# Seven row tiles of a projection phase finished inside the attention that follows

## The reference, cut to what matters

```python
q, k, v, xq = split_cols(h @ w_in, [nh * DIL_HEAD_DIM] * 3 + [D_XA])      # nh = 12 heads of 128
q = apply_rope(rms_norm(hs(q), q_norm), cos, sin)
k = apply_rope(rms_norm(hs(k), k_norm), cos, sin)
for g, (window, dilation) in enumerate(DIL_GROUPS):                       # (128,1), (512,4), (2048,16)
    o, lse = dilated_window_attention(q[g], k[g], v[g], window, dilation)
o = softmax-weighted sum of the three groups
xa = memory_cross_attention(xq, mem_n, xa_w_kv[i], xa_q_norm[i], xa_k_norm[i])   # 4 heads of 64, 256 keys
x = x + concatenate([o, xa]) @ w_out
```

## Time and profile before

| | |
|---|---|
| median of 3 runs | 2404.55 us (2403.34 to 2406.7) |
| the profiled execution | 2405.09 us, its span 2403.3 us |
| PE, DVE, ACT, POOL busy | 2338.1 us (97%), 1888.7 us (79%), 1105.6 us (46%), 221.4 us (9%) |
| seven-block phase, last product | ends at 1514.9 us of the span |
| the first attention on PE | 1527.92 to 1594.02 us |

### The profile page before, as it was taken

The page is one execution under the profiler, slowest core; times in us unless marked ns, Lnnn a source line. Parts: engine busy times, 40 slices in busy tenths (PEclk is TensorE's granted clock), DMA queues, the critical chain, the costliest instruction groups (busy, mean ns, idle before and its releaser), DMA issues. The chain is left out here.

```text
span 2403.3 us, 33350 instructions
## 1 busy us (share of the span) xinstructions
PE 2338.1 (97%) x11988; PEld 2030.3 (84%) x11988; DVE 1888.7 (79%) x2917; ACT 1105.6 (46%) x2217; POOL 221.4 (9%) x252
## 2 busy tenths in 40 slices
PE   8999999999999999999999999798999999999998
PEld 7998877888888888778999999787888888888877
DVE  4422574479999999997998888766779999998996
ACT  6433553344444443446455555665344444444443
POOL 1010012000000002202111111303000000000000
PEclk9999999999999999999999999899999999999999
DMA  4230122222222238963433333745622222227863
GB/s 156 88 98 18 43 86 62 88 72 88 79 79 79 91 112 298 316 199 110 132 113 110 115 106 110 241 139 155 202 82 79 82 94 79 88 79 277 291 184 127
DMA packets 253660, 303.42 MB, mean 126 GB/s; under 512 B 49544, under 2 KB 192888, under 8 KB 253496
## 3 DMA queue, kind: packets, MB, share of 16 engines
q1 hardware_dynamic: 249336, 301.27, 38.2%
q10 hardware_dynamic: 4160, 0.02, 0.1%
HBM read 230.13 MB, written 71.11 MB: 125 GB/s over the span
## 5 line engine op out<-in xcount | busy, mean ns | idle before, releaser
L52 PE MATMUL psum<-f_T_lo 128*128 128x512 f32 x616 | 242.1, 393 | 3.5 <-DVE f_T_lo L698 3.0
L53 PE MATMUL psum<-f_T_lo 128*128 128x512 f32 x616 | 239.9, 389 | 0.0
L54 PE MATMUL psum<-f_T_lo 128*128 128x512 f32 x616 | 239.8, 389 | 0.0
L52 PEld LDWEIGHTS psum<-f_T_lo 128*128 128x128 f32 x616 | 115.6, 188 | 34.5 <-DVE f_T_lo L698 10.8
L52 PE MATMUL psum<-hT_hi,f_up_hi 128*128 128x512 f32 x352 | 137.3, 390 | 0.4 <-DVE f_up_lo L637 0.4
L54 PE MATMUL psum<-hT_hi,f_up_lo 128*128 128x512 f32 x352 | 137.0, 389 | 0.0
L53 PE MATMUL psum<-hT_lo,f_up_hi 128*128 128x512 f32 x352 | 137.0, 389 | 0.0
L54 PEld LDWEIGHTS psum<-f_T_lo 128*128 128x128 f32 x616 | 115.6, 188 | 24.2
L53 PEld LDWEIGHTS psum<-f_T_lo 128*128 128x128 f32 x616 | 115.7, 188 | 23.2
L52 PE MATMUL psum<-p_operand,T_hi 128*128 128x384 f32 x384 | 129.2, 337 | 3.2 <-DVE p_operand L2196 2.5
L54 PE MATMUL psum<-p_operand,token_sums_lo 128*128 128x384 f32 x384 | 128.8, 336 | 0.0
(11 more groups left out here) (501 smaller groups left out, 6674.5 us busy)
## 6 DMA issues: line engine op xcount, KB each, us to landing
raw<-in_ffn_w_up_dram SPq DMA_DIRECT2D x88, 512.0 KB, 4.7
activations<-f_act SPq DMA_DIRECT2D x44, 512.0 KB, 2.6
f_up_pieces<-activations SPq DMA_DIRECT2D x30, 512.0 KB, 5.0
rows_w<-in_b_w_in_dram SPq DMA_DIRECT2D x24, 512.0 KB, 3.8
f_up_pieces<-in_ffn_w_down_dram SPq DMA_DIRECT2D x22, 512.0 KB, 4.8
rows_h<-group_rows SPq DMA_DIRECT2D x14, 768.0 KB, 5.7
group_rows<-raw SPq DMA_DIRECT2D x55, 192.0 KB, 1.8
x_between<-XY SPq DMA_DIRECT2D x16, 512.0 KB, 5.0
```

The costliest lines, as they stand in the source:

```text
L52: nc.tensor.matmul(out, lhs_hi, rhs_hi, start=start, stop=False)
L53: nc.tensor.matmul(out, lhs_hi, rhs_lo, start=False, stop=False)
L54: return nc.tensor.matmul(out, lhs_lo, rhs_hi, start=False, stop=stop)
```

## The change

Tiles 9 to 15 of the last chunk are no longer rotated, scaled and stored in the phase. They stay in their ring slots (tiles 9 to 11 already squared, with their root taken), and the class `LeftOver` treats them inside the first attention: DVE rotates left-over tile n after its other work of step 3n + 2 (steps 2, 5, ... 20), ACT squares the four unsquared ones in steps 3, 5, 7, 9 and scales tile n in step 3n + 4 (4, 7, ... 22), POOL takes two roots behind `CrossNorm`, and SP stores tile n after output tile 2n + 1, and the last three at the end. The k tables are loaded again for them (`left.load`, 2 x 512 KB) into two token tiles of `XY`, behind the stores of tiles 4 and 5. The wait for all stores moves from the opening of the attention to its end. `slots`, `operand0` and `rows_g` get their place in SBUF outside of the phase.

```diff
-LAST_ROTATED_IN = {3: (0, 1), 4: (2, 3), 5: (4, 5), 6: (6, 7, 8, 9, 10, 11), 7: (12, 13, 14, 15)}
+LAST_SQUARED_IN = {2: (0, 1, 2, 3), 5: (4, 5, 6, 7), 6: (8, 9, 10, 11)}
+LAST_ROTATED_IN = {3: (0, 1), 4: (2, 3), 5: (4, 5), 6: (6, 7, 8)}
-LAST_SCALED_IN = {4: (0, 1), 5: (2, 3), 6: (4, 5), 7: (9, 10, 11), 8: (12, 13, 14, 15)}
+LAST_SCALED_IN = {4: (0, 1), 5: (2, 3), 6: (4, 5)}
+LEFT_OVER = (9, 10, 11, 12, 13, 14, 15)
...
                 if m == LASTM - 1:
+                    sp.wait_ge(p_done, product(CH - 1, W22))
+                    left.load(sp)
                     for q in SCALED_LATE:
                         store(CH - 1, q)
                 if m == LASTM:
-                    sp.wait_ge(p_done, product(CH - 1, W22))
...
+class LeftOver:
+    FIRST_SQUARE = 3
...
+    def act(self, act, i):
+        n = (i - 3) // 2 + self.FIRST_SQUARE
+        if i % 2 and self.FIRST_SQUARE <= n < len(LEFT_OVER):
...
+                ins = self.nc.scalar.activation(self.squares_room[:, cols], self.slot(n)[:, cols], ACT.Square, accum_out=self.sums[:, s, 2 * j + h:2 * j + h + 1])
+        n = (i - 4) // 3
+        if i % 3 == 1 and 0 <= n < len(LEFT_OVER):
+            act.wait_ge(self.roped, n + 1)
+            if n >= self.FIRST_SQUARE:
+                act.wait_ge(self.rooted, s + 1)
...
+                ins = self.nc.scalar.activation(self.slot(n)[:, cols], self.slot(n)[:, cols], ACT.Copy, scale=self.rstd[:, s, 2 * j + h:2 * j + h + 1])
+    def dve(self, dve, i):
+        n = (i - 2) // 3
+        if i % 3 != 2 or not 0 <= n < len(LEFT_OVER):
+            return
+        if n == 0:
+            dve.wait_ge(self.loaded, 32)
...
+        for two in range(2):
+            ins = self.nc.vector.tensor_tensor(y[:, :, two, :], x[:, :, 1 - two, :], s[:, 1 - two, :].unsqueeze(1).broadcast_to([P, 2, P // 2]), ALU.mult)
...
+        self.nc.vector.tensor_tensor(heads, heads, self.cos[:, tile].unsqueeze(1).broadcast_to([P, 2, P]), ALU.mult).then_inc(self.turned, 1)
+        dve.wait_ge(self.turned, n + 1)
+        self.nc.vector.tensor_tensor(rows, rows, self.cross(n), ALU.add).then_inc(self.roped, 1)
...
                 if tiles.cross and i == CrossNorm.AT:
                     tiles.cross[2].dve(dve)
+                if left:
+                    left.dve(dve, i)
...
                 tiles.act_next(act, i)
+                if left:
+                    left.act(act, i)
...
                 tiles.cross[2].pool(pool)
+                left.pool(pool)
```

More of the change, by code:

```diff
@@ L1869, in rows_phase @@
                squares_room, small,
-               first_rows, rows_loaded, xq_load, ident, qT, kT):
+               first_rows, rows_loaded, xq_load, ident, qT, kT, first_operand, slot_room, left):
     DH = DC // 2
@@ L1970, in squared_in @@
         def squared_in(m):
-            return due(SQUARED_IN, SQUARED_IN, m)
+            return due(SQUARED_IN, LAST_SQUARED_IN, m)
         def rotated_in(m):
@@ L2312, in _ @@
             for c in range(CH):
-                for quads in ROOTS:
+                for quads in ROOTS if c + 1 < CH else ROOTS[:5]:
                     n, width = root_number(c, quads[0]), 2 * len(quads)
@@ L2489, in dve_next, with attention_phase @@
             self.dve_keys(dve, self.job(i)[0])
-def attention_phase(nc, ph, psum, ident, units, stage, turns_of, row_loads, loads=(), ahead=None, room=(), merge=None):
+def attention_phase(nc, ph, psum, ident, units, stage, turns_of, row_loads, loads=(), ahead=None, room=(), merge=None, left=None, left_store=None):
     U = len(units)
@@ L2690, in _ @@
                 row_loads(sp, t)
+                if left:
+                    for n in range(t // 2, (t + 1) // 2):
+                        left_store(sp, n)
                 if merge and t == 1:
@@ L2699, in _ @@
                 stage.store_sums(sp)
+            if left:
+                for n in range(TT // 2, len(LEFT_OVER)):
+                    left_store(sp, n)
         if ahead is not None:
@@ L4064, in build @@
             rooms = [rows_w[:, i, :].rearrange("p (d n) -> p d n", d=DC // 2) for i in range(4)]
+            with ExitStack() as same_place:
+                raw = sb("first_operand_sum", [P, 2, DC // 2, BLOCK], F32, same_place)
+            with ExitStack() as same_place:
+                x = sb("first_operand", [P, 2, DC // 2, BLOCK], F32R, same_place)
+            first_operand = x[:, 0, :, :], x[:, 1, :, :], raw[:, 1, :, :]
+            rows_g = sb("rows_g", [P, 2, 4 * BLOCK], F32, rows_ctx)
+            slot_room = sb("row_slots", [P, 3, BLOCK], F32, rows_ctx)
+            left = LeftOver(nc, c, raws, slot_room, small_room, squares_room, neg_half, XY[:, TT - 2, :], XY[:, TT - 1, :], tables_d[1])
             rows_phase(nc, "p1", psum, neg_half, hT_hi, hT_lo, h_room, T_hi, sum_lo, sum_room, rooms, raws, begun, w, order, tables_d, rows_d, xq_d, row_stored, squares_room, small_room, lambda t: row_load(0, t), rows_loaded[0],
-                       load_xq, ident, qT, kT)
-            rows_g = sb("rows_g", [P, 2, 4 * BLOCK], F32, rows_ctx)
+                       load_xq, ident, qT, kT, first_operand, slot_room, left)
             stage = Stage(nc, c1, order, outs_d, sums_d)
@@ L4072, in load_rows, with wait_rows, left_store @@
                 sp.dma_start(out, src).then_inc(rows_loaded[n % 2][t], 16)
+            def wait_rows(sp, groups):
+                for s in range(RING):
+                    sp.wait_ge(row_stored[s], 16 * len(range(s, TT + 16 * 2 * groups, RING)))
+            def left_store(sp, n):
+                left.store(sp, n, rows_d[len(order) - 1], row_stored)
+                if n == len(LEFT_OVER) - 1:
+                    wait_rows(sp, len(order))
             def loads_during(n):
@@ L4077, in first @@
                     if t < 0:
-                        for s in range(RING):
-                            sp.wait_ge(row_stored[s], 16 * len(range(s, TT + 16 * 2 * len(order), RING)))
+                        wait_rows(sp, 2)
                     else:
@@ L4117, in turns_of @@
                                      0 if n else TURNED_EARLY, qT, kT, cross)
-                    attention_phase(nc, f"da{n}", psum, ident, units, stage, turns_of, loads_during(n), loads, ahead, room, merge)
+                    attention_phase(nc, f"da{n}", psum, ident, units, stage, turns_of, loads_during(n), loads, ahead, room, merge,
+                                    left if n == 0 else None, left_store)
         up_ctx = ctx.enter_context(ExitStack())
```

59 lines of the change are left out of this document (56 added, 3 removed).

## The result

The changed kernel takes 2412.51 us (median of 7 runs, 2411.22 to 2414.71) against 2404.55 us (7 runs, 2403.34 to 2406.7): 8.0 us more. The ratio is 1.0032, with a 95% interval of 1.0021 to 1.0044. The profiled execution took 2411.91 us, with a span of 2410.1 us against 2403.3.

A forecast was written before the change was run, and what follows sets the result against it. PE, busy 97% of the span, was taken as the bound, so only its waits count. Nine added costs, 11.35 us, less 3.95 gained gave +7.4 on 2404.55: 2412.0 us, range 2404.0 to 2417.5.

The forecast's parts named there:

- the faster case: Rival: `cross_rows` land before 1525, POOL blocks nothing and rotations mostly fit into waits; 2398.5 us, chance 0.09.
- Items 1 to 5: Steps 2 to 5, in order: rotation 1.3, POOL block 2.3, ACT's square 0.35, rotation in key loop 1.3, POOL block 3.05 us.
- Items 1 and 2: Step 2: first rotation stands between sum and mask, 1.3 us; it also waits for POOL's product with the gain, 2.3 us.
- Item 5: Step 5: the second rotation falls inside POOL's second product and waits 3.05 us.
- Item 6: Steps 7 to 9: step 7's square and scaling, 1.2 us, exceed ACT's 0.85 us idle; 0.35 us, step 8's rotation nothing more.
- Items 7 to 9: Rotations: step 11, a key step, 1.3 us; step 14, 1.0 us; steps 17 and 20, 0.4 us at the most.
- item 9: Steps 17 and 20: the rotation's 0.6 us excess over DVE's 0.70 us idle spreads over the next step; 0.4 us at most.
- items 2, 5: Steps 2 and 5: rotations blocked by POOL's first and second products, 2.3 and 3.05 us.
- items 3, 6: ACT's added work: square ahead of an exponential in step 3, 0.35 us; square and scaling in step 7, 0.35 us.
- POOL does not hold up the rotations: Rival: rotations run beside POOL's two products, so both blocks fall away; 2406.6 us, chance 0.26.
- the power too: Rival: POOL's power of 32 columns also blocks the rotations, +5.45 us on the forecast; 2417.5 us, chance 0.09.
- The tables delay the transfer: Rival: the k table loads make `cross_rows` land 2.7 us later; 2414.7 us, chance 0.06.

The follow-up runs named there:

- late rotations: Changed kernel with the left-over rotations, squares and scalings moved to step 17 on, seven stores after the last output tile; 2402.55 us against 2405.69 for the kernel before.
- both repairs: Changed kernel with rotations, squares and scalings from step 17 on and `cross_rows` issued ahead of the `rows_x` loads; 2395.32 us against 2407.51 for the kernel before.
- the first experiment: Changed kernel with POOL's two products over the cross queries cut to 64 of 2048 columns; 2409.18 us against 2405.69 for the kernel before.

## Why the prediction was right, and where it was not

The forecast was 2412.0 and the measurement 2412.51; slower was the likeliest sign, and the two mechanisms, ACT's wait and the rotations behind POOL's products, are the ones that the runs show. That the number fits to 0.5 us is luck. From the landmark the gain ahead of the square was 1.5 us smaller than forecast and the cost behind it 1.0 larger, and a third attention shorter by 2.3, which nobody forecast, made up for both: +7.6 instead of +7.4.

**The start.** Predicted 8.6 us earlier, with `cross_rows` landing 3.95 us earlier, since it is issued so much earlier in SP's queue. From the landmark they were 8.14 and 2.41. In four of the six executions with the changed end of the phase SP issued the first load behind the store of tile 8 at 308.7 us, as worked out (1515.07 is 308.75), and the attention started at 312.4 to 312.6; in two, this one among them, both came 1 us later. So 1 us of the missing 1.5 lies within that scatter; 0.5 is the transfer, which took 12.3 us from issue to landing and not the 11.8 assumed. In absolute times the square at 1529.38 looks like a hit; 1.2 us of it is that the landmark stood earlier in this execution. ACT's wait grew to 7.31, not 5.3: in the profile's own times PE's first scores came 0.7 us sooner than the 1519.3 worked out, ACT was through with steps 0 and 1 in 3.5 us and not in 4.4, and the transfer came 0.4 later than 1529.0. That this wait is the next late thing was right; that moving the one load would nearly remove it was not seen. The prediction named the four `rows_x` loads ahead of it, but only to time the landing and as an argument against the faster case.

**Items 1 to 5, steps 2 to 5.** Counted from the end of ACT's square, the mask of step 6 came at 7.08 us before and 15.53 after: +8.45, where the items give 8.3. Items 1 and 2 hold: the first rotation ended 5.8 us after the square's end (6 predicted). Item 5 was 1.2 too large, with 1.88 us (2.36 - 0.48) instead of 3.05, because the copy ahead of it ended late, at 12.3 instead of 11.05. The likely reason is the cost taken at nothing, PE's lower clock: its work in steps 3 to 5 ran at 0.50, and what that cost was time that DVE would have been blocked in anyway. With `cross_rows` first, where PE was at 0.50 for a shorter time, the copy ended at 11.5 and item 5 measured 2.74.

**Item 6.** The key copy of step 11 stood at 17.04 before and 25.69 after, +8.65. The items up to 6 give 8.65.

**Items 7 to 9, and the clock.** The first maximum of a cross unit, 5 steps ahead of the one shown in the earlier trace rows, stood at 24.82 before (1559.74) and 35.65 after (1566.97): +10.83, where items 1 to 8 give 10.95. From there to the second attention the change added 1.5 us (36.66 - 35.14) and not the 0.4 of item 9. The second drop of the clock, at 1568 to 1571, falls there. The two experiments nearest to this kernel (POOL's products small, `cross_rows` first) had the same 1.61 us gap and no drop, and took 35.35 both. So item 9 measured 0.2, and the drop 1.3. The mis-sized term of the sum is thus the clock, bounded at 0 to 1 us and taken at nothing. No run switches the clock alone, so its share is read from the windows and from this comparison of profiles, and was not tested.

**The whole behind the square.** The stretches of the table take the 12.35 us apart:

| | us | from | forecast |
|---|---|---|---|
| rotations, their own time | 5.3 | POOL's products small, less no rotations | items 1, 4, 7, 8, 9: 5.3 |
| POOL's blocks | 4.1 | after, less POOL's products small, up to the first maximum | items 2, 5: 5.35 |
| ACT's squares and scalings | 1.1 | no rotations, less late rotations, up to the first maximum | items 3, 6: 0.7 |
| what the long wait leaves behind | 0.6 | late rotations, less both repairs, up to the first maximum | 0 |
| second drop of the clock | 1.3 | after, less POOL's products small, behind the first maximum | 0 |

The fourth row compares two kernels that differ by the order of the loads alone; behind the square the one with the long wait has PE at 0.50 for some 5 us and the other does not, so the lower clock is the likely cause. The rows form a chain of differences from the kernel after to the one before, and so add up to the whole; that each is worth the same in every kernel is an assumption.

**The third attention**, of which the prediction said that all that follows is shifted by the same. It gave back 2.3 us, and that hid the 2.5 (9.94 - 7.4) by which the second attention started later than forecast. Before, DVE's small merge products met POOL's splitting of `w_out`: 2.36 us beside POOL's 2.36, and just ahead of them 1.04 us for a maximum of 8 columns beside POOL's conversion of 1.04:

```profile
1652.63 1.04 DVE L3479 TENSOR_TENSOR merge_top<-merge_tops 128x8 f32<-128x8 f32 x1
```

```profile
1652.61 1.04 POOL L1168 CAST o_w_hi<-raw 128x1024 fp32r<-128x1024 f32 x1 [0.41 <-DMA raw<-in_b_w_out_dram]
```

After, POOL's operations stood elsewhere and the same maximum and the same three products took

```profile
1661.38 0.16 DVE L3583 TENSOR_TENSOR merge_top<-merge_tops 128x8 f32<-128x8 f32 x1
...
1661.77 0.32 DVE L3586 TENSOR_TENSOR merge_tops<-merge_tops,merge_top 128x8 f32<-128x8 f32 x3
```

between POOL's

```profile
1658.80 2.36 POOL L1170 TENSOR_TENSOR o_w_lo<-raw,o_w_hi 128x1024 fp32r<-128x1024 f32 x1
1662.50 1.04 POOL L1168 CAST o_w_hi<-raw 128x1024 fp32r<-128x1024 f32 x1 [1.34 <-DMA raw<-in_b_w_out_dram]
```

In the eight profiles the third attention lasts 48.4 to 48.9 us in the four where the three products took 2.36 or 2.37, and 46.5 to 46.7 in the four where they took 0.32. POOL's third piece waits for a load (0.3 to 0.5 us in the first four, 1.3 to 1.8 in the others), so whether it meets DVE's step looks like luck of that load's arrival. I had quoted the blocked rows as evidence and not asked what would become of them. No kernel moved that splitting by itself, so the cause rests on this sorting and on the same blocking as shown in the first experiment; it was not tested.

**The rivals.** "POOL does not hold up the rotations" is refuted by the first experiment, and "the power too" by the 0.42 and 0.45 us of the instructions beside it. "The tables delay the transfer" fails: issued at 1509.06 and 1509.53, they landed within 3.8 to 4.6 us, by 1514.1, ahead of the first `rows_x` load at 1514.89; and `cross_rows` started ACT 11.7 us after its issue in the first experiment and 11.8 in the late one, as before. "Faster" asked for a landing before 1525 and no blocking; landing at 1522 with blocking gave 2406.65, and only with the rotations moved did it come, larger than the -6 that I gave it.

## What to carry to other kernels

When a tail is taken away from ahead of a barrier, look at what the next engine waits for after it, and issue that transfer ahead of the ones that nobody needs yet: 1 MB behind 3 MB cost 6 us here, for a change of two lines. Work moved into another phase should go where its engine has slack in every step, not where its step is a loop's only link: the same seven rotations cost 9.4 us in steps 2 to 20, POOL's blocks included, and 0.2 in steps 17 to 29. Before putting a DVE operation with two inputs in SBUF somewhere, read what POOL does at that time; and look for places downstream where the two already collide, since a shift changes those too.

## What the runs showed of the hardware

- DVE's products with both inputs in SBUF stood still for the length of POOL's products of 2048 columns: 2.70 and 2.36 us against 0.48. DVE's reduction of one SBUF tile beside the same POOL product was not held up: 2.29 us in both kernels, and 2.29 in the first experiment too, where POOL's product took 0.32. The Trainium skill, page "SBUF — State Buffer", section "SBUF: two separate sides", describes such an exclusive lock for the whole instruction, and the products agree with it.
- By that section of the Trainium skill every GpSimd operation that reads SBUF takes part. POOL's power of 32 columns (5.43 to 5.58 us) did not hold up DVE's sums and products of 0.42 to 0.45 us beside it in any of these runs. The measurement decides: here the power did not block them, or only for a small part of its time.
- POOL's CAST of 1024 columns holds DVE up as well: a DVE maximum of 8 columns that took 0.16 us elsewhere took 1.04 beside it, and 0.47 to 0.75 in three experiments where it began later beside the same CAST; in all four it ended within 0.02 us of the CAST's end.
- The granted clock fell to 0.50 within PE's idle time of 7.97 us and stayed there until 1544, through steps in which PE worked only in part. After the same 1.61 us gap it fell in one kernel and not in two others. After the gap of 2.05 to 2.19 us at the barrier it fell in three of the six executions with the early start (to 0.63 in 1520 to 1522 with POOL's products small, 0.55 in 1522 to 1524 with late rotations, 0.60 in 1518 to 1520 with both repairs), and stayed at 1.00 up to their next long gap in the other three, the changed kernel among them.
- The stretch ahead of the landmark differed by up to 5.6 us between executions of kernels whose work is the same up to there. In the two latest ones (1210.70 and 1209.17) the granted clock of the window from 350 to 400 us is 0.83, in the six others 0.93. Absolute times of two profiles should be compared from a landmark close to the change.
